# Two edges of a one-core transformer layer: x loaded in column halves around the first weight half, and the last output tile finished in pieces

## The reference

```python
h = rms_norm(x, g_attn)
z = h @ w_in                    # q, k, v of two attentions, an indexer, two gates
o_a, o_b = moba_attention(...), dsa_attention(...)
x = x + (sigmoid(ga) * (o_a @ w_br_a) + sigmoid(gb) * (o_b @ w_br_b)) @ w_out
x = x + hier_moe(rms_norm(x, g_ffn), ...)      # 32 experts, 2 per token
x = x + sigmoid(rms_norm(x, g_ple) @ w_ple_gate) * (p @ w_ple_proj)
return rms_norm(x, g_final)
```

## Time and profile before

| | us |
|---|---|
| median of 3 executions | 1030.96 |
| lowest, highest | 1030.13, 1032.24 |
| profiled execution | 1032.11 |
| its span in the trace | 1030.3 |
| TensorE busy | 973.2 |
| VectorE, ScalarE, GpSimd busy | 382.6, 309.4, 144.7 |

### The profile page before, as it was taken

One profiled execution on the slowest core, in us unless ns is written; L12 is line 12 of the kernel. 1 busy time (PEld: TensorE's weight loads), 2 busy tenths in 40 slices (PEclk: granted clock), 3 DMA queues, 4 the chain that ended last, 5 costly groups with the idle time before them and its releaser, 6 DMA issues.

```text
span 1030.3 us, 11949 instructions
## 1 busy us (share of the span) xinstructions
PE 973.2 (94%) x4770; PEld 595.3 (58%) x4770; DVE 382.6 (37%) x778; ACT 309.4 (30%) x530; POOL 144.7 (14%) x141
## 2 busy tenths in 40 slices
PE   5999999999999999998999999999999999999696
PEld 4776787576688888885434444444333344443474
DVE  4225697655453536336121111111101111032875
ACT  5334424746432214241111111111111111212564
POOL 0202123836600000000000100000000000010300
PEclk8999999999999999998999999999999999999799
DMA  8422131000072250855899999999999999999501
GB/s 308 151 82 82 41 97 33 1 2 1 2 281 87 87 196 3 326 207 194 333 422 419 421 420 420 421 420 420 421 421 420 420 420 417 419 421 412 206 21 62
DMA packets 58376, 256.04 MB, mean 249 GB/s; under 512 B 12094, under 2 KB 12734, under 8 KB 33232
## 3 DMA queue, kind: packets, MB, share of 16 engines
q1 hardware_dynamic: 49456, 248.26, 60.2%
q0 software_dynamic: 2560, 4.20, 1.1%
q10 hardware_dynamic: 6304, 2.80, 1.0%
HBM read 248.95 MB, written 10.49 MB: 252 GB/s over the span
## 4 chain that ended last, share of the span: by engine, by line
PE 74%; DMA 15%; DVE 5%; ACT 2%; POOL 2%; issue 1%; SPq 0%; ACTq 0%; DVEq 0%; POOLq 0%
PE psum L701 36%; PE psum L1035 17%; DMA slot<-in_w_up 13%; PE psum L992 4%; PE psum L1054 4%; PE psum L1053 3%; PE psum L1071 1%; PE psum L1011 1%; PE psum L886 1%; PE psum L871 1%; DMA pair_in<-pair_rows 1%; PE psum L1001 1%; PE psum L859 1%; PE psum L847 1%; DVE ple_gate_lo L1830 1%
## 5 line engine op out<-in xcount | busy, mean ns | idle before, releaser
L1035 PE MATMUL psum<-slot,xt 128*64 128x512 f32 x512 | 238.8, 611 | 14.7 <-DMA slot<-in_w_up 12.4
L1036 PE MATMUL psum<-slot,xt 128*64 128x512 f32 x512 | 239.1, 611 | 0.0
L1035 PEld LDWEIGHTS psum<-slot,xt 128*64 128x64 f32 x512 | 67.1, 139 | 142.0 <-issue 136.5
L701 PE MATMUL psum<-w_hi,act_hi 128*128 128x512 f32 x288 | 115.5, 401 | 6.1 <-DVE w_lo L556 6.1
L2026 POOL DMA_INDIRECT pair_rows<-y,slot_pair x30 | 31.2, 1041 | 627.5 <-ACT y L1369 627.5
L1053 PE MATMUL psum<-slot,ht 128*64 128x512 f32 x256 | 115.8, 595 | 1.2 <-DVE ht L1856 1.2
L1054 PE MATMUL psum<-slot,ht 128*64 128x512 f32 x256 | 115.9, 596 | 0.0
L701 PE MATMUL psum<-w_lo,act_hi 128*128 128x512 f32 x288 | 113.1, 393 | 0.0
L701 PE MATMUL psum<-w_hi,act_lo 128*128 128x512 f32 x288 | 112.7, 391 | 0.0
L556 DVE TENSOR_TENSOR w_lo<-raw,w_hi 128x2048 fp32r<-128x2048 f32 (+1 forms) x31 | 70.5, 2275 | 84.1 <-ACT w_hi L551 84.0
L1362 ACT ACTIVATE small<-psum,slot_inv 64x512 f32<-64x512 f32 x32 | 21.9, 684 | 256.3 <-PE psum L1036 255.2
(11 more groups left out here) (278 smaller groups left out, 1476.6 us busy)
## 6 DMA issues: line engine op xcount, KB each, us to landing
slot<-in_w_gate SPq DMA_DIRECT2D x64, 1024.0 KB, 23.4
slot<-in_w_up SPq DMA_DIRECT2D x64, 1024.0 KB, 24.6
slot<-in_w_down SPq DMA_DIRECT2D x64, 1024.0 KB, 24.0
raw<-in_w_in SPq DMA_DIRECT2D x22, 1024.0 KB, 5.1
raw<-in_w_out SPq DMA_DIRECT2D x4, 1024.0 KB, 5.1
slot<-in_w_ple_gate SPq DMA_DIRECT2D x4, 1024.0 KB, 20.0
pair_in<-pair_rows SPq DMA_DIRECT2D x4, 1024.0 KB, 14.5
rows_tok<-in_x SPq DMA_DIRECT2D x4, 512.0 KB, 6.9
```

The source lines that it names most:

```text
L701: mms = [pe.matmul(ps, a, b, start=first and n == 0, stop=last and n == 2) for n, (a, b) in enumerate(ops)]
L1035: mm_g = pe.matmul(ps[FIRST:2 * FIRST, :], left, g[:, k, :], start=first, stop=last)
L1036: mm_u = pe.matmul(ps[0:FIRST, :], left, u[:, k, :], start=first, stop=last)
```

## The change

In the head: the identity is issued first. x comes in two column halves, each as four DMAs of 256 KB (`load_x`); the second half of x is issued when the first weight half has landed, and stands ahead of the second weight half in SP's queue. TensorE transposes the first half, runs ten products of the identity with itself that nobody reads, and starts the first product; in its first token tile each k tile waits for its own `act_lo` alone (`ready`), and after that token tile stand the 16 transposes of x's second half. ScalarE and VectorE split weight half 0 in quarters, one ahead of each of the k tiles 0 to 3; half 1 is now split between tiles 3 and 4. ScalarE does a small copy at its start. `square_x` waits for the whole of x.

In the tail, for the last token tile alone: the second column half's product is made as two of 256 columns (`tail_pieces`), the second in bank 5, with sigmoid, product with the projection, sum and squares in the same pieces. Ahead of the last piece's squares ScalarE takes a square root of a constant, so the table changes there. The scaling and the output are done in two column halves. The semaphores `pe_steps` and `pool_steps`, which nobody waits on, become one.

```diff
-        sp.dma_start(stage_tok[:, 0], x_v[:, 0]).then_inc(x_in[0], 16)
+        def load_x(h):
+
+            for t in range(NT):
+                sp.dma_start(stage_tok[:, t, h * 512:(h + 1) * 512], x_v[:, t, h * 512:(h + 1) * 512]
+                             ).then_inc(x_rest_in if h else x_in[t], 16)
+
         sp.dma_start(cst[:, 0:P], const[:, 0:P]).then_inc(ident_in, 16)
-        for t in range(1, NT):
-            sp.dma_start(stage_tok[:, t], x_v[:, t]).then_inc(x_in[t], 16)
+        load_x(0)
         for n, s in enumerate(HALVES):
             load(n, source(s))
+            if n == 0:
+                sp.wait_ge(raw_loaded[0], 16)
+                load_x(1)
             if n == 1:
                 sp.dma_start(cst[:, P:], const[:, P:]).then_inc(const_in, 16)
 
...
         out_v = out[0].rearrange("(t p) d -> p t d", p=P)
-        for t in range(NT):
+        for t in range(NT - 1):
             sp.wait_ge(last_out, t + 1)
             sp.dma_start(out_v[:, t], xres[:, t]).then_inc(out_done, 16)
-        sp.wait_ge(out_done, 16 * NT)
+        for h in range(2):
+            sp.wait_ge(last_out, NT + h)
+            sp.dma_start(out_v[:, NT - 1, 512 * h:512 * h + 512], xres[:, NT - 1, 512 * h:512 * h + 512]).then_inc(out_done, 16)
...
-        def half_product(s, left, k0, then=None):
+        def half_product(s, left, k0, then=None, ready=None):
 
             n, k_n, last = HALF_OF[s], tiles_in(s), last_half(s)
-            pe.wait_ge(lo_done, n + 1)
+            if ready is None:
+                pe.wait_ge(lo_done, n + 1)
             hi, lo = [half_view(v[n], n, k_n) for v in (w_hi_at, w_lo_at)]
             w = hi.shape[2]
             for t in range(NT):
...
                 for k in range(k_n):
+                    if ready and t == 0:
+                        ready(k)
                     l_ = [v[:, k0 + k, t * P:(t + 1) * P] for v in left]
...
-        def turn_x_in():
-
+        def turn_x_in(h):
+
+            if h:
+                pe.wait_ge(x_rest_in, 16 * NT)
             for t in range(NT):
-                pe.wait_ge(x_in[t], 16)
-                for k in range(KD):
+                if h == 0:
+                    pe.wait_ge(x_in[t], 16)
+                for k in range(4 * h, 4 * h + 4):
                     mm = pe.transpose(bank[k][:, t * P:(t + 1) * P], stage_tok[:, t, k * P:(k + 1) * P], ident)
                     if t == NT - 1:
                         mm.then_inc(bank_filled[k], 1)
...
                 if a in ROPES and i == 0:
                     pe.wait_ge(roped, ROPES.index(a) + 1)
                 transposes(s, [stage_z[:, STAGE[a], t, i * P:(i + 1) * P] for t in range(NT)])
             elif kind == "z":
-                if a == "iq":
-                    for k in range(4 * i, 4 * i + 4):
+                if (a, i) == ("iq", 1):
+                    for k in range(4, KD):
                         drained(pe, ("turn", "h", k))
+                if (a, i) == ("iq", 0):
+                    half_product(s, (act_hi, act_lo), 0, lambda t: turn_x_in(1) if t == 0 else None,
+                                 lambda k: drained(pe, ("turn", "h", k)))
+                    return
                 if a != "ix":
                     half_product(s, (act_hi, act_lo), 4 * i, (lambda t: beside_z(s, t)) if s in BESIDE_Z else None)
                     return
...
         def gate_tail(t, n):
 
-            ps = bank[4 + 2 * (t % 2) + n]
-            if t >= 2:
-                pe.wait_ge(tail_gated, 2 * (t - 2) + n + 1)
...
+            for j, a, b in tail_pieces(t, n):
+                a, b = a - 512 * n, b - 512 * n
+                ps = tail_bank(j, t, n)[:, a:b]
+                if j == 2 * NT:
+                    pe.wait_ge(tail_gated, 2 * (t - 1) + n + 1)
+                elif t >= 2:
+                    pe.wait_ge(tail_gated, 2 * (t - 2) + n + 1)
+                for i in range(2):
...
+                    hi, lo = (v[PLE_GATE.index((n, i))][:].rearrange("p (k n) -> p k n", k=4) for v in (gate_hi, gate_lo))
+                    for k in range(4):
+                        _, mm = three(ps, (tail_hi[:, t % 2, 4 * i + k, :], tail_lo[:, t % 2, 4 * i + k, :]),
+                                      (hi[:, k, a:b], lo[:, k, a:b]), (i, k) == (0, 0), (i, k) == (1, 3))
+                mm.then_inc(tail_filled, 1)
...
         def square_x():
 
+            act.wait_ge(x_rest_in, 16 * NT)
             for t in range(NT):
...
                         act.wait_ge(gain_in, 16)
+                        act.wait_ge(raw_loaded[0], 16)
+                    if i < 4:
+                        ins = act.copy(w_hi_at[0][:, i * 512:(i + 1) * 512], raw_at[0][:, i * 512:(i + 1) * 512])
+                    if i == 3:
+                        ins.then_inc(hi_done, 1)
                     act.activation(act_hi[:, i, :], ps, ACT.Copy, scale=g_in[:, i:i + 1]).then_inc(turn_hi, 1)
...
         act.wait_ge(eps_set, 1)
+        act.activation(spare[:], eps[:, 0:1], ACT.Copy, scale=eps[:, 0:1])
+        act.wait_ge(eps_set, 1)
...
-            if s in (("turn", "h", 3), ("turn", "h", KD - 1)):
-                split_high(act, 0 if s[2] == 3 else 1)
+            if s == ("turn", "h", 3):
+                split_high(act, 1)
             if s == ("turn", "h", KD - 1):
                 square_x()
...
+        def last_square(t, n, part=0):
+            j, a, b = tail_pieces(t, n)[part]
+            act.wait_ge(added, j + 1)
+            act.activation(tail_junk[t][:, a:b], xres[:, t, a:b], ACT.Square, accum_out=ssq_tail[:, j - 2 * t, t:t + 1]
+                           ).then_inc(last_squared, 1)
...
+        def sigmoid(t, n, part=0):
+            j, a, b = tail_pieces(t, n)[part]
+            a, b = a - 512 * n, b - 512 * n
...
+            act.wait_ge(tail_filled, j + 1)
...
             sigmoid(t, 1)
-            last_square(t)
+            last_square(t, 0)
+            last_square(t, 1)
+            if t == NT - 1:
+                sigmoid(t, 1, 1)
+                act.activation(table_of_root[:], eps[:, 0:1], ACT.Sqrt)
+                last_square(t, 1, 1)
             last_root(t)
...
                     dve.wait_ge(gain_in, 16)
+                    dve.wait_ge(raw_loaded[0], 16)
+                if i < 4:
+                    at = slice(i * 512, (i + 1) * 512)
+                    ins = dve.tensor_tensor(w_lo_at[0][:, at], raw_at[0][:, at], w_hi_at[0][:, at].bitcast(F32), ALU.subtract)
+                if i == 3:
+                    ins.then_inc(lo_done, 1)
                 dve.scalar_tensor_tensor(out=act_lo[:, i, :], in0=bank[b], scalar=g_in[:, i:i + 1],
...
-            if s in (("turn", "h", 3), ("turn", "h", KD - 1)):
-                split_low(dve, 0 if s[2] == 3 else 1)
+            if s == ("turn", "h", 3):
+                split_low(dve, 1)
             if s == ("turn", "h", KD - 1):
                 invert_x()
...
         def add_gated(t, n):
-            dve.wait_ge(tail_gated, 2 * t + n + 1)
-            g = small[:, 2 * (t % 2) + n, :]
-            link(dve.tensor_tensor(g, g, proj_sb[:, n, t, :], ALU.mult))
-            dst = xres[:, t, 512 * n:512 * n + 512]
-            dve.tensor_tensor(dst, dst, g, ALU.add).then_inc(added, 1)
+            for j, a, b in tail_pieces(t, n):
+                dve.wait_ge(tail_gated, j + 1)
+                g = small[:, 2 * (t % 2) + n, a - 512 * n:b - 512 * n]
+                link(dve.tensor_tensor(g, g, proj_sb[:, n, t, a - 512 * n:b - 512 * n], ALU.mult))
+                dst = xres[:, t, a:b]
+                dve.tensor_tensor(dst, dst, g, ALU.add).then_inc(added, 1)
...
-            dve.scalar_tensor_tensor(out=xres[:, t], in0=xres[:, t], scalar=cols[5], in1=g_last, op0=ALU.mult, op1=ALU.mult
-                                     ).then_inc(last_out, 1)
+            for at in [slice(0, 512), slice(512, D)] if last else [slice(0, D)]:
+                dve.scalar_tensor_tensor(out=xres[:, t, at], in0=xres[:, t, at], scalar=cols[5], in1=g_last[:, at],
+                                         op0=ALU.mult, op1=ALU.mult).then_inc(last_out, 1)
```

54 lines of the change are left out of this document (28 added, 26 removed).

## The result

| | before | changed |
|---|---|---|
| median (range) of 5 runs each | 1030.96 us (1030.13 to 1034.29) | **1023.95 us** (1021.6 to 1026.45) |
| profiled execution | 1032.11, span 1030.3 | 1023.95, span 1022.2 |
| ratio | | **0.9932, 95% interval 0.991 to 0.9954** |

The change is faster by 7.0 us (the interval says 4.7 to 9.3). The forecast was 5.0 us and 1026.0; the time lies at the lower end of its range. Where the two traces differ tells which terms held.

The account below looks back on a forecast made before the run. TensorE, busy 94% of the span, was taken as the bound, so only its standstills at head and end counted. Head 3.4 plus tail 1.6 save 5.0 us: 1030.96 - 5.0 = 1026.0, range 1023.6 to 1029.6.

Parts of the forecast that it names:

- First weight half in at 10.6: Head, transfers: with 1.05 MB less ahead of it, the first weight half lands at 10.6 us, between 8.6 and 11.5.
- doesn't land earlier: Rival, head: the queues' pause is a delay of its own, half lands at 13.0, head saves 1.0, 1028.4 us; 9%.
- Pairs 1.27 apart, product 17.1 us after the half: Head: VectorE sets 1.27 us a pair; first product done at 27.7 in place of 31.1, 3.4 us saved.
- The clock stays up: Head, first product: identity products leave no long gap, so TensorE's granted clock is 1.00 from 13 to 30 us.
- the rival's price: Rival, head: clock stays low through the first product, costing 9.4 us, 1035.4 in all; 3%.
- Covers: Head: slack of later-issued work before it is wanted: 3.4 us for tile 7, 1.4 for the inverse of x's squares.
- Carried to the end: Between head and end: TensorE's order and freed buffers pace the loads, so the head's 3.4 us stay saved.
- Small transfers pay each: Rival, head: x's second half pays 2.6 us for each of four DMAs, 3.2 us later, 1029.2; 5%.
- The end, 1.6 us: Tail: last product in pieces, table load covered, halved scaling save 1.0 us; the halved output saves 0.6.
- 256 columns cost as 512: Rival, tail: a 256-column matmul takes the 512-column pitch, 0.2265 us; tail -3.4, 1031.0 us in all; 6%.
- the sum itself: Whole kernel: head 3.4 plus tail 1.6 make 5.0 us saved, 1026.0 us for the median.
- The chances by class: Whole kernel, against a 2.1 us measurement limit: 0.83 faster by more, 0.13 within it, 0.04 slower.

## Why the prediction came out as it did

- **First weight half in at 10.6.** Measured 10.80. The estimate from bytes ahead of it held; that it "doesn't land earlier" fell.
- **Pairs 1.27 apart, product 17.1 us after the half.** Measured 1.26 apart and 28.2 - 10.8 = 17.4. The head saved 3.0 of the forecast 3.4: 0.2 from the landing, 0.3 from the three steps ahead of the first product (it started at 13.64, not 13.2).
- **The clock stays up.** It did, and without the identity products TensorE ran at half pace until the transposes. But the rival's price was for a low clock through all 48 matmuls; what the missing products cost was 0.8 us.
- **Covers.** They held by less than I had counted. The last block of x's second half landed at 17.03 (forecast 14.8), wanted at 18.1; act_lo of tile 7 was done at 26.7 (24.3), wanted at 28.2, since the second weight half's cast began at 19.79 (17.3). Both are SP's wait: without it the block is in at 13.56 and the cast begins at 16.28. The inverse of the squares was late: the first tile's scaling behind the product moved by 2.0 us only, the next by 3.0, and nothing waited for it.
- **Carried to the end.** Held: 3.0 to 3.1 at 55 us and at 955. "Small transfers pay each" fell: without the wait x's four late blocks landed 0.68 us apart (11.52 to 13.56), with it 0.83 to 1.39, not 2.6. The figures that the prediction names there from the Trainium skill, "DMA: Bandwidth & Descriptors", sections "Anatomy of one DMA" and "Bandwidth", are stated there for DMAs that GpSimd issues; these are SyncE's.
- **The end, 1.6 us.** Measured 1.6, with 0.120 a matmul, 1.1 up to the scaling (forecast 1.0) and 0.5 in the output (0.6). That 256 columns cost as 512 fell. By the load time that the Trainium skill gives, "TensorE: Matmul & The Clock Gate", section "LDWEIGHTS (loading the stationary operand)", 107 ns for 128 columns, the pieces would by estimate have ended 0.6 us earlier: as the spacing of 256-column matmuls the measured 0.120 decides against it.
- **The step that failed** is the sum itself, by a term that it doesn't have: it stopped at "in between, TensorE's order and the buffers that it frees pace the loads", and took the 950 us between head and end as unchanged. 3.5 us of the profiled 8.1, and some 2 of the measured 7.0, came from there, from an addition and a sum that no longer run in the wrong order. The row was to be seen in the trace of before (3.03 us for an addition that elsewhere takes 1.21), but the prediction reads no row between 700 and 991 us. By its own test, "Wrong, if the span between the first 40 us and the last 16 changes by over 1 us", that part was wrong. The two sums are right (3.0 of 3.4 and 1.6 of 1.6), and with them the sign. That the time still lies inside the range, by 0.35 us, is luck: the range was wide enough on the side where an effect fell that it didn't know of. The chances by class are added wrongly: from the rivals' own they are at most 0.80 for faster, and 0.17 and 0.03 for the others, not 0.83, 0.13 and 0.04.

## What to carry to other kernels

Before a sum is made, look through the groups for an instruction whose longest instance is twice its shortest: where VectorE and GpSimd work at once on the same memory, who begins first was worth 3.6 us here, and an edit elsewhere, even five idle instructions, turned the order. Put such work on one engine or behind a wait; both made the kernel before faster (4.8 and 3.6 us). Split and reorder what feeds the first product so that the pacing engine (here VectorE) never waits for something it doesn't need yet; ordering issues on one queue did that job without a wait.
